# Low parts without squares in between, an earlier exponent table and an output head ahead of the last sums, in a two-layer transformer kernel

## The reference

```
h     = rmsnorm(x, norm_gain)
proj  = h @ w_in                  # q k v z b a of the delta group, q k v z of the attention group
o_dn  = gated_delta_rule(...)     # 4 heads; here 4 chunks of 128 tokens, each in two halves of 64
o_dn  = rmsnorm(o_dn, gain) * silu(z)
o_df  = softmax attention with two maps per head, the second weighted with -lambda; 4 heads
o_df  = rmsnorm(o_df, gain) * (1 - lambda_init) * silu(z)
x     = x + concat(o_dn, o_df) @ w_out
```

## Time and profile before

| | |
|---|---|
| median of three runs | 2025.61 us |
| the profiled execution | 2024.86 us, span 2023.1 us |
| instructions | 30232 |
| TensorE, its weight loads | 1992.5 us (98%), 1703.2 us (84%) |
| VectorE, ScalarE, GpSimd | 864.0, 734.1, 936.2 us |
| granted TensorE clock, mean | 0.998 |

### The profile page before, as it was taken

The page is one execution under the profiler, slowest core; times in us unless marked ns, Lnnn a source line. Parts: engine busy times, 40 slices in busy tenths (PEclk is TensorE's granted clock), DMA queues, the critical chain, the costliest instruction groups (busy, mean ns, idle before and its releaser), DMA issues.

```text
span 2023.1 us, 30232 instructions
## 1 busy us (share of the span) xinstructions
PE 1992.5 (98%) x11374; PEld 1703.2 (84%) x11374; DVE 864.0 (43%) x1507; ACT 734.1 (36%) x1113; POOL 936.2 (46%) x1220
## 2 busy tenths in 40 slices
PE   8999999999999999999999999999999999999998
PEld 6788777799999999788998888888888888888887
DVE  7844675922222224994442244333334452222112
ACT  4643554432222224534444242333333332232222
POOL 5432112555445565553332635454544665555564
PEclk9999999999999999999999999999999999999999
DMA  5211101222222323221111322222222222223232
GB/s 178 94 63 43 42 32 43 73 84 93 93 87 90 104 93 105 76 94 61 63 64 42 122 72 89 73 99 74 81 81 76 92 93 93 99 89 102 94 104 84
DMA packets 49898, 168.68 MB, mean 83 GB/s; under 512 B 6416, under 2 KB 8592, under 8 KB 49808
## 3 DMA queue, kind: packets, MB, share of 16 engines
q1 hardware_dynamic: 46336, 161.37, 23.4%
q10 hardware_dynamic: 3472, 6.03, 0.9%
HBM read 165.29 MB, written 2.10 MB: 83 GB/s over the span
## 4 chain that ended last, share of the span: by engine, by line
PE 87%; DVE 9%; ACT 2%; issue 1%; DMA 1%; DVEq 0%; ACTq 0%
PE slot L2055 86%; DVE ix_score L1860 1%; DVE top L1856 1%; DVE ix_score L1877 1%; DVE square L1813 1%; DVE x_lo L1830 0%; DVE xt L1822 0%; DMA ix_rot<-rotations 0%; PE slot L2492 0%; PE slot L2230 0%; PE slot L2195 0%; DVE ak L1815 0%; DMA small<-small_in 0%; ACT mixed_hi L945 0%; DVE aq L1815 0%
## 5 line engine op out<-in xcount | busy, mean ns | idle before, releaser
L2569 POOL TENSOR_TENSOR w_lo<-w_raw,w_hi 128x256 fp32r<-128x256 f32 x1216 | 936.0, 802 | 1076.2 <-ACT w_hi L824 816.6
L2055 PE MATMUL slot<-x_hi,w_hi 128*128 128x264 f32 (+1 forms) x1864 | 642.9, 345 | 0.2 <-DVE x_lo L1830 0.2
L2055 PE MATMUL slot<-x_hi,w_lo 128*128 128x264 f32 (+1 forms) x1864 | 629.8, 338 | 0.0
L2055 PE MATMUL slot<-x_lo,w_hi 128*128 128x264 f32 (+1 forms) x1864 | 628.1, 337 | 0.0
L2055 PEld LDWEIGHTS slot<-x_hi,w_hi 128*128 128x128 f32 x1864 | 351.2, 188 | 46.6 <-issue 7.6
L2055 PEld LDWEIGHTS slot<-x_lo,w_hi 128*128 128x128 f32 x1864 | 350.5, 188 | 38.6
L2055 PEld LDWEIGHTS slot<-x_hi,w_lo 128*128 128x128 f32 x1864 | 351.3, 188 | 37.5 <-issue 1.4
L824 ACT ACTIVATE w_hi<-w_raw 128x1024 fp32r<-128x1024 f32 x215 | 225.3, 1054 | 320.5 <-PE slot L2055 312.0
L2055 PE MATMUL slot<-f_hi,w_hi 128*128 128x264 f32 (+2 forms) x550 | 173.7, 316 | 0.0
L2055 PE MATMUL slot<-f_hi,w_lo 128*128 128x264 f32 (+2 forms) x550 | 173.5, 315 | 0.0
L2055 PE MATMUL slot<-f_lo,w_hi 128*128 128x264 f32 (+2 forms) x550 | 173.1, 315 | 0.0
(11 more groups left out here) (348 smaller groups left out, 2862.0 us busy)
## 6 DMA issues: line engine op xcount, KB each, us to landing
w_raw<-weights SPq DMA_DIRECT2D x303, 512.0 KB, 3.2
h<-x_t ACTq DMA_DIRECT2D x4, 512.0 KB, 6.4
dec<-decays ACTq DMA_DIRECT2D x4, 264.0 KB, 3.0
const<-consts SPq DMA_DIRECT2D x1, 576.0 KB, 7.1
at_rot<-rotations ACTq DMA_DIRECT2D x1, 528.0 KB, 5.0
ix_rot<-rotations ACTq DMA_DIRECT2D x1, 528.0 KB, 6.9
rt_rot<-rotations ACTq DMA_DIRECT2D x1, 528.0 KB, 3.9
w_raw<-weights SPq DMA_DIRECT2D x2, 256.0 KB, 4.2
```

The source lines that it names most:

```text
L2055: return nc.tensor.matmul(out, lhsT, rhs, start=start, stop=stop)
L2569: nc.gpsimd.tensor_tensor(w_lo[j][:, piece], w_raw[j][:, piece], w_hi[j][:, piece].bitcast(F32), ALU.subtract).then_inc(s_lo, 1)
```

## The change

Five edits.

- **First blocks.** VectorE makes the eight low parts with nothing in between; all eight squares are ScalarE's, and `w_split(1)` and `w_split(2)` stand ahead of squares 0 and 2. ("norm", 0) goes from behind ("qkv", 1) to behind ("qkv", 2).
- **Head norms.** `norm_point` steps on until the sum lies at none of the points 17, 0 and 1 of a chunk: heads 0 and 1 move from points -1 and 36 to 1 and 37. With the new stretches heads 3 and 6 move from 53 and 47 to 50 and 46; heads 2, 4, 5 and 7 stay at 43, 1, 39 and 55.
- **Matmul units.** The stretches end one and two points earlier: the attention's last queries and keys are done at point 52, not 54, and 29 units are left behind point 53, not 34.
- **Table.** Behind the last gate of point 29 ScalarE loads `LN_EXP`.
- **Output heads.** Head 4 is gated on VectorE behind point 71, and its high part made on ScalarE ahead of the copy of ("o", 3), for which the last probabilities' copy of point 71 moves ahead too; points 72 and 73 lie behind head 5 on VectorE. TensorE multiplies head 4 ahead of and between the two late sums, and heads 5, 6, 0 and 1 one after the other over four columns.

```diff
@@ results, and tensor
-        if j == 1:
+        if j == 2:
             add(("norm", 0))
@@
-STRETCHES = [(8, -2, -2), (6, -1, -1), (82, 0, 38), (16, 39, 46), (16, 47, 54), (32, 55, 70)]
+STRETCHES = [(8, -2, -2), (6, -1, -1), (82, 0, 38), (16, 39, 45), (16, 46, 52), (32, 53, 70)]
@@ norm_point
-    return p + 1 if (p + 1) % POINTS == POINTS - 1 else p
+    while (p + 1) % POINTS in (POINTS - 1, 0, 1):
+        p += 1
+    return p
@@ scalar, first blocks
-                elif k == KD - 1:
-                    w_split(2)
-            for k in range(SQUARES_VECTOR, KD):
+            for k in range(KD):
+                if k in (0, 2):
+                    w_split(1 + k // 2)
                 nc.scalar.activation(squares0[k], h[:, k, TQ], ACT.Square).then_inc(s_sq, 1)
@@ scalar, all_squares, behind the gate of point 29
                         act.sem_inc(s_silu, 1)
+                        nc.scalar.preload_act_table_set(LN_EXP)
+                        made["table"] = LN_EXP
@@ scalar, end of a chunk
                 for _ in range(4):
                     aside()
+                if n == NQ - 1:
+                    aside()
+                    x_high(1, 4, M, mixed_hi)
                 wait_result(act, ("o", n))
...
-                aside()
+                if n < NQ - 1:
+                    aside()
             while point[0] < LAST_POINT:
                 aside()
             A.sync()
             squares_chunk(3)
+            x_high(1, 5, M, mixed_hi)
             wait_evac(act, ("PV", DF_H - 1, NQ - 1))
             squares([dqk[:, 3, :]])
+            x_high(1, 6, M, mixed_hi)
             rsqrt(("ho", 3), 1.0 / P, T)
-            for i in (4, 5, 6):
-                x_high(1, i, M, mixed_hi)
             rsqrt(("ho", 7), 1.0 / P, T)
@@ vector, first blocks
-                if 0 <= k - 3 < SQUARES_VECTOR:
-                    V.own(nc.vector.tensor_tensor(squares0[k - 3], h[:, k - 3, TQ], h[:, k - 3, TQ], ALU.mult))
             for k in range(1, KD):
-                if k >= SQUARES_VECTOR:
-                    dve.wait_ge(s_sq, k + 1 - SQUARES_VECTOR)
-                V.sync()
+                dve.wait_ge(s_sq, k + 1)
+                if k > 1:
+                    V.sync()
@@ vector, behind the last chunk
-            while point[0] < LAST_POINT:
-                aside()
...
+                    elif i == 5:
+                        wait_result(dve, ("o", NQ - 1))
+                    elif i == 6:
+                        while point[0] < LAST_POINT:
+                            aside()
...
-            for part in (HEADS_OUT[0:3], HEADS_OUT[3:KD]):
+            for part in (HEADS_OUT[0:1], HEADS_OUT[1:3], HEADS_OUT[3:KD]):
@@ tensor, output
-            for i in LATE_HEADS:
-                sums(("ho", i), 1, T)
             for j in range(4):
-                out_part(j, 0, 3)
+                out_part(j, 0, 1)
+                if j % 2:
+                    sums(("ho", LATE_HEADS[j // 2]), 1, T)
+            for i in range(1, 5):
+                for j in range(4):
+                    out_part(j, i, i + 1)
             for j in range(4):
-                out_part(j, 3, KD)
+                out_part(j, 5, KD)
```

More of the change, by code:

```diff
@@ L308 @@
 IX_STEPS = (NQ - 1) * 4
-SQUARES_VECTOR = 4
 WARMING = 4
@@ L2067, in sums @@
                     q = done["sq"]
-                    pe.wait_ge(s_sq, KD - SQUARES_VECTOR + q + 1)
+                    pe.wait_ge(s_sq, KD + q + 1)
                     if w == T:
```

## The result

| | before | changed |
|---|---|---|
| median, runs on the same chip | 2025.95 us (12 runs) | 2030.94 us (12 runs) |
| span of the profiled execution | 2023.1 us | 2027.9 us |
| granted TensorE clock, mean | 0.998 | 0.996 |
| ratio | | 1.0024, 95% interval 1.0016 to 1.0032 |

The changed kernel is 5.0 us slower: inside the range, 3.4 us above the forecast of 2027.5, and just over the bound of 0.2% within which I had put most of the chance. The intervals in this document use fast executions alone, and the one slow execution of experiment 12, like the one of the kernel before beside experiments 8 to 11, moves a median by 0.2 us at most.

What follows compares the result with a forecast made beforehand. The prediction took TensorE, busy 98% of the span, as the bound. Its terms, +3.1 + 2.2 - 1.4 - 2.0 = +1.9 us, on 2025.6 gave 2027.5 us, with an 8-in-10 range of 2022.5 to 2032.

Steps and rivals of the forecast that it cites:

- the clock behind the wait for block 3: First blocks: after some 5.5 us of TensorE idle, one fall to the low clock, charged at 1.6 us.
- squares off VectorE: First blocks: block 1 starts 2.2 us sooner and the old low-clock stretch, 1.6 us, goes: -3.8 us.
- norm behind block 2: First blocks: nothing covers the wait for block 3, TensorE idles some 5.5 us and the clock falls once: +6.9 us.
- first blocks together: Start of the kernel: earlier block 1 against the later norm, net +3.1 us, bounds +0.9 and +5.8.
- first head norm, chunk 0: Start of chunk 0: ScalarE's table load, logarithm and exponential become exposed, +2.2 us, bounds +1.5 and +2.65.
- chunks 2 and 3: Table preload and moved norms shorten waits, matmul units shift from chunk 3 to 2: -1.4 us, bounds -2.6 and +0.5.
- output heads: Kernel end: four columns finish 4.2 us earlier, but VectorE's feeding keeps only 2.0: -2.0 us, bounds -1.0 and -4.2.
- rival (2): Slower: TensorE stays at the low clock after the wait for block 3, adding 3.2 us, 2030.7 us; chance 0.30.
- the overlap of 0.43: Chunk 0: part of the wait at 111.50 that the moved sum takes along, subtracted from 2.65 us exposed.
- Rivals (3): Faster: block 3's high half isn't behind the norm, or its wait is hidden, 2020.6 us; chance 0.15.
- (4): Head norms' shift is neutral and chunk 0 hides the table load: 2025.3 us, inside the first case's chance.
- within 0.2%: Likeliest case: the four terms hold over the whole kernel, 2023 to 2029.6 us; chance 0.55.

Runs made afterwards that it cites:

- experiment 12: Changed kernel plus 21 matmuls without effect on the output, put behind the norm to fill TensorE's wait for block 3: 2027.45 us.
- experiment 8: Kernel before with VectorE's four squares given to ScalarE and the second block's high half ahead of them, norm still behind block 1: 2022.52 us.
- experiment 9: Kernel before with squares on ScalarE, table load and output heads' edits; norm, points and stretches as they were: 2019.42 us.
- experiment 10: Kernel before with one edit, the norm's sum behind block 2 instead of block 1: 2034.19 us.
- experiment 11: Kernel before with one edit, the first head norm from point -1 to point 1: 2029.20 us.
- experiment 3: Changed kernel with the first head norm back at point -1: 2026.83 us.
- experiment 4: Changed kernel with the norm behind block 1 again and the first head norm at point -1 again: 2020.38 us.
- experiment 5: Kernel before with only the added table load behind the gate of point 29: 2024.01 us.
- experiment 6: Kernel before with the output heads' new order alone: 2023.44 us.
- experiment 7: Kernel before with the new points and stretches, first head norm left at -1, no table load added: 2026.54 us.
- experiment 1: Changed kernel with the norm behind block 1 again, all squares still on ScalarE: 2022.27 us.
- experiment 2: Changed kernel with block 3's high half made ahead of ScalarE's reciprocal root, norm left behind block 2: 2027.79 us.

## Why the prediction was right, and what it mis-sized

The mechanism of the forecast was right: the four places and the waits came as stated (in chunk 0 one step sooner and with another releaser), and the time fell in the range. Two of its terms were too small: the clock behind the wait for block 3, 1.6 us forecast and 2.6 to 2.7 in the rows, and chunk 0, 2.2 forecast and 3.6 in the profile.

The single edits on the kernel before add up to what the whole change does: -3.3 (squares), +8.4 (norm), +3.4 (first head norm), -1.8 (table), +0.7 (points), -2.4 (output heads) make +5.0. Each has its interval of 2 us or more to either side, so the exact agreement is luck. The gains and losses of 3 us and more stand clear of the noise; the sign of the points' 0.7 does not, and that of the table's 1.8 rests on its rows.

| term, us | predicted | two profiles compared | single edits |
|---|---|---|---|
| squares off VectorE | -3.8 | | -3.3 |
| norm behind block 2 | +6.9 | | +8.4; undone -8.7 |
| first blocks together | +3.1 | +4.15 | +5.1 |
| first head norm, chunk 0 | +2.2 | +3.6 | +3.4; undone -4.1 |
| chunks 2 and 3 | -1.4 | -1.1 | -1.1 |
| output heads | -2.0 | -1.8 | -2.4 |
| sum | +1.9 | +4.8 | +5.0 |

The third column comes from shifts of rows: 66.68 to 70.83; 121.85 to 129.60 less that; 350.24 to 355.69 with the 1.18 us of its wait put back, 6.6, less 7.75; and the span's 4.8 less 6.6. It carries the clock of two single executions, which is uncertain by 1 to 2 us a profile. The 3.1 of the forecast was a fall of 3.8 and a rise of 6.9.

- **First blocks, steps right.** Block 1 at 17.52 (17.5 expected), the wait for block 3 with its start at 34.94 (34.93) and its releaser. The last low part ended at 15.05 instead of 14.4, as it took 1.23 us beside GpSimd, but block 1 waited for GpSimd, not for it. Block 1 was not ready at 16.9, which the prediction had worked out for GpSimd alone: GpSimd's pieces were slowed too, six of them in 6.45 us, where four took 2.84 us in the earlier trace rows. Beside each other both engines pay.
- **First blocks, the size that failed.** "I charge one fall at the same 1.6". That was the price of 3.3 us at the low level behind a loosely busy TensorE. Around 5.3 us of standing still it was 6.8 us in three profiles of three (the changed kernel, experiments 3 and 10), of which TensorE worked through 5.2 to 5.7. That is 2.6 us from block 3 to the multiply, which with the 1.5 of block 3 makes the 4.15 measured against 3.1, and filling the wait took 2.7 us of it away. So rival (2) named the mechanism but made it too dear: it added 3.2 us where about 1.0 was missing. That its number, 2030.7, is nearly the median is luck: of the 2.9 us by which the profile's 4.8 misses the forecast, chunk 0 has 1.4 and the last two terms 0.5.
- **Chunk 0.** The order cost about 2.6 us against 2.2: the table load fell due at 123.02 in front of both norms, and the overlap of 0.43 that I subtracted gave little or nothing. The other 1.0 in the changed kernel's profile is a fall of the clock behind the wait of 2.07 us, which the forecast hadn't thought of. The Trainium skill, "ScalarE: Activation LUTs", section "What ACT_TABLE_LOAD costs", would have the chunk at 3.6 by the prediction's estimate, with its drain of 1.38 us. The shift was indeed 3.6, but for another reason: 1.0 of it is the clock, and the logarithm starts at 124.31, 0.01 us behind the load's end, so no drain shows.
- **Chunks 2 and 3.** The sum held and its split only partly: the table load was worth 1.8, not 2.6, as 0.56 us of the wait remains; the points cost 0.7, not 1.2, by a median that can't tell these two apart. The kernel with the old points (experiment 9) stood 1.0 below experiment 4, on the same side.
- **Output heads.** Right in place and, within the interval, in size. The waits for the last low parts came back in front of the first gate block as expected, 1.99 us, and took the rest of the gain.
- **Rivals (3) and (4)** are out: the wait for block 3 is there in full, and chunk 0 hides none of the load. The 0.55 for "within 0.2%" rested on one fall of the clock at its old price as the usual case; in the three profiles with this wait the low time was twice that each time.

What stays open: why the same 2 us of waiting was followed by a fall in some profiles and not in others. Nothing was run that varies it alone.

## What to carry to other kernels

When a sum or a norm is moved behind another block of matmuls, ask what stands behind its follow-up in the other engines' queues: here the next weights, and making one of them earlier only moved the stall to the next one. A stall of TensorE must be priced as its length plus what the clock loses afterwards (2.7 us behind 5.3 here), and where good edits come together with changes of order, each is to be tried without the others (11.5 us here).

## What the runs showed of the hardware

- **The low clock is not the same in each execution.** The five profiles with the same first blocks as the kernel before (before, experiments 5, 6, 7 and 11) have granted clocks of 0.99 and 0.84, 0.89 and 0.77, 0.75 and 0.73, 0.87 and 0.79, 1.00 and 1.00 in the stretches 10 to 20 and 20 to 30 us: 3.4, 6.8, 10.4, 6.8 and 0 us low. TensorE's norm starts at 27.02, 28.16, 28.48, 27.95 and 26.15. A profile of one execution can thus be 1 to 2 us off the median by this alone, which is as large as the terms in question.
- **The new first blocks are low less often, but not never.** The eight profiles with all squares on ScalarE have 0 us low in these two stretches (the changed kernel, experiments 4, 8 and 12) or 3.4 us (experiments 1, 2, 3 and 9). Experiments 1 and 4 have the same first blocks: the norm starts at 24.64 in one and at 23.45 in the other.
- **With 5.3 us of idle the fall came each time, with 2 us seldom.** The wait of 5.3 us had 6.8 us of low clock in three profiles of three, of which 1.2 to 1.7 lie in the wait itself; the wait of 4.55 us in experiment 2 had 3.4 us. The wait of 2.05 to 2.09 us in chunk 0 was followed by a fall in the changed kernel and by none in experiments 1, 2, 11 and 12; the one of 1.97 us in chunk 2 by one in experiment 11 and by none before and in experiments 6, 8 and 10.
- **Here idle, not the work behind it, brought the low clock.** With matmuls whose results nobody uses in the gap the clock stayed at 1.00 over the same blocks (experiment 12, one profile; the medians agree).
